# Latent attention: rotated score products on two row halves, the rotation's last sum on GpSimd, scores by pairs of heads in four banks

## The reference, cut to what matters

```
cq = rms_norm(x @ w_dq, q_norm_g)
q = (cq @ w_uq).reshape(b, s, H, MLA_NOPE + MLA_ROPE)      # H 8, NOPE 128, ROPE 64
ckv_kr = x @ w_dkv
ckv = rms_norm(ckv_kr[..., :MLA_KV_LORA], kv_norm_g)
kv = (ckv @ w_ukv).reshape(b, s, H, MLA_NOPE + MLA_V)
k_nope, v = kv[..., :MLA_NOPE], kv[..., MLA_NOPE:]
q_rope = apply_rope(q[..., MLA_NOPE:], cos[:, None, :], sin[:, None, :])
k_rope = apply_rope(ckv_kr[..., MLA_KV_LORA:], cos, sin)
sc = (einsum('bqhd,bkhd->bhqk', qn, k_nope) + einsum('bqhr,bkr->bhqk', qr, k_rope)) * scale
p = softmax(sc, -1)
o = einsum('bhqk,bkhd->bqhd', p, v)
out = o.reshape(b, s, H * MLA_V) @ w_o
```

## Time and profile before

| | us |
|---|---|
| median of 3 runs | 1151.84 |
| lowest, highest | 1151.42, 1151.96 |
| the profiled execution | 1151.98 |
| its span in the profile | 1150.2 |
| latent attention, scores to the output projection's first matmul | 53.48 to 75.81 |

### The profile page before, as it was taken

One profiled execution on the slowest core, in us unless ns is written; L12 is line 12 of the kernel. 1 busy time (PEld: TensorE's weight loads), 2 busy tenths in 40 slices (PEclk: granted clock), 3 DMA queues, 4 the chain that ended last, 5 costly groups with the idle time before them and its releaser, 6 DMA issues.

```text
span 1150.2 us, 19057 instructions
## 1 busy us (share of the span) xinstructions
PE 1135.3 (99%) x6617; PEld 981.3 (85%) x6617; DVE 804.2 (70%) x1230; ACT 700.7 (61%) x1233; POOL 50.9 (4%) x73
## 2 busy tenths in 40 slices
PE   9999999999999999999999999999999999999997
PEld 7987888888899878888888888888998888888886
DVE  5866888888756578888886655656657657655655
ACT  6665766766566666676665555556585655555553
POOL 0100000000100000000001000000000320000000
PEclk9999999999999999999999999999999999999999
DMA  7705666756344455666654765655783005876761
GB/s 247 247 7 149 186 200 199 217 179 214 128 130 148 164 147 174 211 205 195 202 176 133 216 205 171 208 151 139 217 269 121 2 21 163 231 206 171 205 156 63
DMA packets 237173, 194.75 MB, mean 169 GB/s; under 512 B 11230, under 2 KB 219712, under 8 KB 237120
## 3 DMA queue, kind: packets, MB, share of 16 engines
q1 hardware_dynamic: 237040, 194.01, 56.2%
q10 hardware_dynamic: 80, 0.03, 0.0%
HBM read 192.97 MB, written 1.05 MB: 169 GB/s over the span
## 4 chain that ended last, share of the span: by engine, by line
PE 94%; DVE 3%; ACT 1%; POOL 1%; issue 1%; DMA 0%; POOLq 0%; DVEq 0%; ACTq 0%
PE psum L853 26%; PE psum L858 14%; PE psum L884 7%; PE psum L887 7%; PE psum L891 7%; PE psum L667 6%; PE psum L669 6%; PE psum L668 6%; PE psum L723 1%; PE psum L1388 1%; DVE resid_eps L2119 1%; PE psum L841 1%; POOL st L584 1%; PE psum L1136 1%; PE psum L845 1%; PE psum L842 1%
## 5 line engine op out<-in xcount | busy, mean ns | idle before, releaser
L853 PE MATMUL psum<-act_hl,hi_u 128*128 128x512 f32 x1312 | 326.5, 391 | 0.0
L2041 DVE TENSOR_TENSOR lo_u<-raw_u,hi_u 128x2048 fp32r<-128x2048 f32 x103 | 236.1, 2292 | 93.0 <-ACT hi_u L1493 54.4
L853 PEld LDWEIGHTS psum<-act_hl,hi_u 128*128 128x128 f32 x1312 | 240.6, 188 | 46.2
L858 PEld LDWEIGHTS psum<-act_hl,lo_u 128*128 128x128 f32 x1312 | 179.0, 190 | 12.8
L858 PE MATMUL psum<-act_hl,lo_u 128*128 128x256 f32 x1312 | 183.0, 282 | 0.0
L1613 ACT ACTIVATE arena<-psum 128x256 f32<-128x256 f32 x174 | 64.9, 377 | 123.6 <-PE psum L858 114.2
L2180 DVE TENSOR_TENSOR arena<-psum,arena 128x256 f32<-128x256 f32 x174 | 73.0, 422 | 93.7 <-ACT arena L1613 93.3
L1511 ACT ACTIVATE hi_u<-raw_u 128x2048 fp32r<-128x2048 f32 x68 | 129.7, 1907 | 11.7 <-DMA raw_u<-in_ffn_w_gu 11.7
L2046 DVE TENSOR_TENSOR lo_d<-raw_d,hi_d 128x1024 fp32r<-128x1024 f32 x88 | 106.7, 1216 | 8.6 <-ACT hi_d L1520 8.6
L2190 DVE SCALAR_TENSOR_TENSOR arena<-arena,vecs 128x255 f32<-128x255 f32 x176 | 85.0, 483 | 37.9 <-ACT arena L1621 26.8
L2013 DVE TENSOR_TENSOR lo_u<-raw_u,hi_u 128x1024 fp32r<-128x1024 f32 (+6 forms) x84 | 78.2, 971 | 28.2 <-ACT hi_u L1490 28.0
(11 more groups left out here) (311 smaller groups left out, 1811.8 us busy)
## 6 DMA issues: line engine op xcount, KB each, us to landing
raw_u<-in_ffn_w_up SPq DMA_DIRECT2D x88, 512.0 KB, 5.6
raw_d<-in_ffn_w_down SPq DMA_DIRECT2D x86, 512.0 KB, 3.4
raw_u<-in_ffn_w_gu SPq DMA_DIRECT2D x84, 512.0 KB, 5.7
raw_u<-in_diff_w_qkv SPq DMA_DIRECT2D x24, 512.0 KB, 4.5
raw_u<-in_w_in SPq DMA_DIRECT2D x24, 512.0 KB, 4.5
raw_u<-in_mla_w_o SPq DMA_DIRECT2D x8, 512.0 KB, 4.5
raw_u<-in_diff_w_o SPq DMA_DIRECT2D x8, 512.0 KB, 3.9
raw_u<-in_w_out SPq DMA_DIRECT2D x8, 512.0 KB, 4.5
```

Source lines behind the costliest of these rows:

```text
L853: pe.matmul(o, hi[:, k, :], act_hl[:, k].rearrange("p a t -> p (a t)"), start=k == 0, stop=False)
L858: mm = pe.matmul(o[:, SEQ:], lo[:, k, :], act_hl[:, k, 0, :], start=False, stop=k == KC - 1)
L2041: dve.tensor_tensor(v[0], v[1], v[2].bitcast(F32), ALU.subtract).then_inc(S("lo_u_done"), 1)
```

## The change

- The rows of `m_qr` are now ordered by head first: rows 0 to 63 are the even head of a pair, rows 64 to 127 the odd one. The shared rotated keys stand in one tile `m_kr` with a copy in each half. The zeros, their memset on DVE and three of ACT's four copies are gone.
- The rotated products have 64 rows each (`m_qr[r, ...]`, `m_kr[r, :]`) and alternate between the two halves, with the results of the two heads in two banks.
- The rotation's sum moves from DVE to GpSimd. It is cut into four pieces of 32 rows for each of the four steps, since the pieces change their rows; each piece waits for the one before. DVE waits for GpSimd before it overwrites the buffers `t1` and `t2` two steps later. PE waits for DVE's three products (`m_qr_parts`) where it waited for the sum, and for all 16 pieces ahead of the first scores.
- `scores` makes two heads at once: first four products with `m_q`, then four half-height ones. The banks are 0, 1, 2, 7 instead of 0, 1, 2. PE's loop becomes: scores of pair `p`, `turn(2p-2)`, `values(2p-3)`, `turn(2p-1)`, `values(2p-2)`. The loops of DVE and ACT still go head by head in the order given above.

```diff
-        m_kr = ar(3072, 2, SEQ)
+        m_kr = ar(3072, SEQ)
+        m_bank = [0, 1, 2, 7]
...
+            pool.wait_ge(S("slopes"), 8)
+            for i in range(4):
+                pool.wait_ge(S("m_qr_parts"), 3 * i + 3)
+                t1, t2 = qr2[:, i % 2, 0], qr2[:, i % 2, 1]
+                for h in range(2):
+                    for j in range(2):
+                        src, dst = (slice(at, at + 32) for at in (64 * j + 32 * h, 64 * h + 32 * j))
+                        pool.tensor_tensor(m_qr[dst, i, :], t1[src], t2[src], ALU.add).then_inc(S("m_qr_out"), 1)
+                        pool.wait_ge(S("m_qr_out"), 4 * i + 2 * h + j + 1)
...
-                def scores(h):
-                    if h >= 3:
-                        pe.wait_ge(S("m_exp"), 2 * (h - 2))
+                def scores(p):
+                    if p >= 2:
+                        pe.wait_ge(S("m_exp"), 4 * (p - 1))
+                    o = lambda h, t: psum[:, m_bank[h % 4], t * SEQ:t * SEQ + SEQ]
+                    for h in range(2 * p, 2 * p + 2):
+                        for t in range(TT):
+                            pe.matmul(o(h, t), m_q[:, h, tok(t)], m_k[:, h, :], start=t == 0, stop=False)
                     for t in range(TT):
-                        o = psum[:, h % 3, t * SEQ:t * SEQ + SEQ]
-                        pe.matmul(o, m_q[:, h, tok(t)], m_k[:, h, :], start=True, stop=False)
-                        mm = pe.matmul(o, m_qr[:, h // 2, tok(t)], m_kr[:, h % 2, :], start=False, stop=True)
-                    mm.then_inc(S("m_scores"), 1)
+                        for e in range(2):
+                            r = slice(ROPE * e, ROPE * e + ROPE)
+                            mm = pe.matmul(o(2 * p + e, t), m_qr[r, p, tok(t)], m_kr[r, :], start=False, stop=t == 1)
+                            if t:
+                                mm.then_inc(S("m_scores"), 1)
...
-                pe.wait_ge(S("memsets"), 3)
+                pe.wait_ge(S("m_qr_out"), 16)
-                for i in range(H):
-                    scores(i)
-                    if i == 2:
+                for p in range(H // 2):
+                    scores(p)
+                    if p == 0:
                         pe.wait_ge(S("m_k_out"), 2)
                         pe.wait_ge(S("m_v_out"), 2)
-                    if i >= 2:
-                        turn(i - 2)
-                    if i >= 3:
-                        values(i - 3)
+                    else:
+                        turn(2 * p - 2)
+                        if p >= 2:
+                            values(2 * p - 3)
+                        turn(2 * p - 1)
+                        values(2 * p - 2)
...
-                        for e in range(2):
-                            for r in (slice(32 * e, 32 * e + 32), slice(64 + 32 * e, 96 + 32 * e)):
-                                act.activation(m_kr[r, e, :], psum[r, 3, 0:SEQ], ACT.Copy).then_inc(S("m_kr_out"), 1)
+                        act.activation(m_kr, psum[:, 3, 0:SEQ], ACT.Copy).then_inc(S("m_kr_out"), 1)
...
-                        dve.wait_ge(S("m_qr_out"), i - 1)
+                        dve.wait_ge(S("m_qr_out"), 4 * (i - 1))
...
-                    ch.wait()
-                    dve.tensor_tensor(m_qr[:, i, :], t1, t2, ALU.add).then_inc(S("m_qr_out"), 1)
```

More of the change, by code:

```diff
@@ L381, in program @@
         kr3 = normed[:].rearrange("p a b -> p (a b)")[:, 1280:1664].rearrange("p (a t n) -> p a t n", a=3, t=TT)
-        kr_twice = normed[:].rearrange("p a b -> p (a b)")[:, 1664:1920].rearrange("p (t c e n) -> p t c e n", t=TT, c=2, e=2)
+        kr_twice = normed[:].rearrange("p a b -> p (a b)")[:, 1664:1920].rearrange("p (t e c n) -> p t c e n", t=TT, c=2, e=2)
+        kr_rows = normed[:].rearrange("p a b -> p (a b)")[:, 1664:1920].rearrange("p (t n) -> p t n", t=TT)
         qr2 = masks[:].rearrange("p (i a b) t -> p i a (b t)", i=2, a=2)
@@ L972, in mla @@
                     if i >= 2:
-                        pe.wait_ge(S("m_qr_out"), i - 1)
+                        pe.wait_ge(S("m_qr_parts"), 3 * (i - 1))
                     high_products(*turned[:1], u, *turned[1:], 0, [0], True)
@@ L994, in mla @@
                         for t in range(TT):
-                            mm = pe.transpose(psum[:, 3, t * P:t * P + P], kr_twice[:, t].rearrange("p c e n -> p (c e n)"), ident[:])
+                            mm = pe.transpose(psum[:, 3, t * P:t * P + P], kr_rows[:, t, :], ident[:])
                         mm.then_inc(S("latent_tr"), 1)
@@ L1004, in mla @@
                     if i == 0:
-                        pe.wait_ge(S("m_kr_out"), 4)
+                        pe.wait_ge(S("m_kr_out"), 1)
                     else:
                         pe.wait_ge(S("m_q_out"), 4)
-                        pe.wait_ge(S("m_qr_out"), 4)
+                        pe.wait_ge(S("m_qr_parts"), 12)
                     keys = [psum[:, 4 * i + h // 2, (h % 2) * SEQ:(h % 2) * SEQ + SEQ] for h in range(4)]
@@ L1750, in mla @@
                         for t in range(TT):
-                            act.activation(m_p[:, i % 3, t, :], psum[:, i % 3, t * SEQ:t * SEQ + SEQ], ACT.Exp,
+                            act.activation(m_p[:, i % 3, t, :], psum[:, m_bank[i % 4], t * SEQ:t * SEQ + SEQ], ACT.Exp,
                                            scale=M_SCALE, bias=soft[:, i, 1, t:t + 1],
@@ L2288, in mla @@
                     if i >= 2:
-                        dve.wait_ge(S("m_qr_out"), i - 1)
+                        dve.wait_ge(S("m_qr_out"), 4 * (i - 1))
                     dve.wait_ge(S("used_u"), U_UQ + i + 1)
                     raw = psum[:, 5 + 2 * (i % 2), 0:SEQ]
-                    ch.put(dve.tensor_tensor(t1, raw, ropeq[:, 0, :], ALU.mult))
+                    dve.tensor_tensor(t1, raw, ropeq[:, 0, :], ALU.mult).then_inc(S("m_qr_parts"), 1)
                     for c in range(2):
                         src, dst = slice(64 * c, 64 * c + 64), slice(64 - 64 * c, 128 - 64 * c)
-                        ch.put(dve.tensor_tensor(t2[dst], raw[src], ropeq[src, 1, :], ALU.mult))
-                    ch.wait()
-                    dve.tensor_tensor(m_qr[:, i, :], t1, t2, ALU.add).then_inc(S("m_qr_out"), 1)
+                        dve.tensor_tensor(t2[dst], raw[src], ropeq[src, 1, :], ALU.mult).then_inc(S("m_qr_parts"), 1)
                     split_u(U_UQ + i + 2)
@@ L2308, in mla @@
                         dve.wait_ge(S("m_scores"), i + 1)
-                        ch.link(dve.tensor_reduce(soft[:, i, 0, 0:2], psum[:, i % 3, :].rearrange("p (t k) -> p t k", t=2),
+                        ch.link(dve.tensor_reduce(soft[:, i, 0, 0:2], psum[:, m_bank[i % 4], :].rearrange("p (t k) -> p t k", t=2),
                                                   AX, ALU.max))
@@ L2574, in _ @@
             dve.memset(resid_eps[:, :, D:], ROOT_D * EPS ** 0.5).then_inc(S("memsets"), 1)
-            dve.memset(m_kr, 0.0).then_inc(S("memsets"), 1)
             norm_first()
```

1 line of the change is left out of this document (removed).

## The result

| | before | after |
|---|---|---|
| median, us | 1151.68 | 1155.51 (1154.98 to 1155.69) |
| span of the profiled execution | 1150.2 | 1153.2 |
| scores' first to output projection's first matmul | 22.33 | 24.23 |
| first scores wait for GpSimd | none | 1.30 |

The changed kernel takes 1.0031 times as long as the one before, with a 95% interval from 1.0022 to 1.0040: **3.8 us slower**. That is outside the predicted range, which ended at 1154.2. The two profiled executions (1151.98 and 1154.98) differ by 3.0 us.

The account below looks back on a forecast made before the run. PE bounds the score stretch: waits of 3.91 us, less 0.3 of old waits and 2.64 saved on products, give +0.97, taken as +1.0, with GpSimd's sum and the projections at 0. From 1151.84: 1152.8 us, range 1150.9 to 1154.2.

Parts of the forecast that it names:

- GpSimd's sum: Rotation's sum on GpSimd: 16 pieces at 0.72 us each, hidden by the projections, so costing nothing.
- Stretched by 1.51/1.05: GpSimd's pieces beside a busy DVE: 1.00 us each, ending at 51.6, before PE's need at 53.4.
- the threshold of 1.11: GpSimd's pieces: above 1.11 us each, (53.4 - 35.6)/16, the cover by the projections is gone.
- The row: Trace of a 512-element GpSimd addition, 1.05 us beside idle DVE and 1.51 beside busy, used for the pieces' stretch.
- GpSimd's sum is late: Rival before the first scores: pieces exclude DVE's splits or exceed 1.11 us, 3.4 us late, 1156.2 us; chance 0.10.
- all 9.7 us of splits: DVE's two-input splits up to 53.4 us; full exclusion would leave GpSimd 8.1 us for 11.5 of pieces.
- The products: Half-height rotated products in the scores: 1.07 us a pair in place of 1.73, saving 2.64 over four pairs.
- The 0.21 us that I charged for going in and out: Scores of each pair: 0.21 us lost entering and leaving the half-height form, included in the 1.07.
- 0.97: Lower bound for a pair's half-height products, half of the second layer's 1.93 us; takes 0.3 off the time.
- The waits: PE's waits for DVE and ACT in the paired scores' stage: 3.91 us in all, against 0.3 before.
- turn(1): PE's transposes of head 1, after DVE scales it: start at 60.84 after a wait of 1.17 us.
- The projections: Stage before the scores: GpSimd's work slows DVE's splits within slack, so 0, bounds -0.2 and +0.5 us.

Follow-up runs that it names:

- fine_waits: The changed kernel, with scores of each pair waiting only for that pair's GpSimd pieces instead of all 16; 1153.75 us, ratio 1.0017.
- turned_first: The changed kernel, with DVE scaling the odd head before the next maximum and ACT copying turned probabilities before the next even head's exponentials; 1153.84 us, ratio 1.0017.
- gpsimd_only: The kernel before, with only the rotation's sum moved to GpSimd, as one 128-row addition a step in the old row order; 1151.91 us, ratio 0.9999.

## Why the prediction was wrong, point by point

1. **GpSimd's sum: the step that failed.** "Stretched by 1.51/1.05 it is 1.00 each, to 51.6: still in time." The piece by itself was nearly right, though by a guess between two rows: 0.72 with its wait, 0.73 and 0.08 of wait measured. Sixteen of them would have ended at 47.9. The stretch was not right. Two of GpSimd's additions in the kernel after, beside DVE's products from PSUM:

```profile
L632 POOL TENSOR_TENSOR arena<-masks x2: 731/736/740, 41.0 to 41.8; 32x256 f32<-32x256 f32 x2
```

Three more, and the splits that each of them meets, from the timelines of POOL and DVE:

```profile
42.58 1.70 POOL L632 TENSOR_TENSOR arena<-masks 32x256 f32<-32x256 f32 x1
44.36 1.59 POOL L632 TENSOR_TENSOR arena<-masks 32x256 f32<-32x256 f32 x1
51.15 1.60 POOL L632 TENSOR_TENSOR arena<-masks 32x256 f32<-32x256 f32 x1
...
42.47 1.23 DVE L2029 TENSOR_TENSOR lo_u<-raw_u,hi_u 128x1024 fp32r<-128x1024 f32 x1
43.61 1.76 DVE L2029 TENSOR_TENSOR lo_u<-raw_u,hi_u 128x1024 fp32r<-128x1024 f32 x1
...
50.84 1.31 DVE L2029 TENSOR_TENSOR lo_u<-raw_u,hi_u 128x1024 fp32r<-128x1024 f32 x1
```

Beside a long split a piece takes 2.2 to 2.4 times as long, not 1.44 times. The mean came to 1.21 us against the threshold of 1.11 that the prediction itself had worked out. The row was a bad bound: an addition of 512 columns, which had run for 0.80 us when DVE's one instruction with two inputs in SBUF began beside it (889.87 and 890.67). The cost was 1.46 us (54.56 less 53.10) where I had 0, and fine_waits gives 1.76 back and measures 1153.75, inside the predicted range: without this step the time lies inside it. The rival "GpSimd's sum is late" held 0.10 and 3.4 us. It came with under half of that.
The Trainium skill (SBUF — State Buffer, Who interferes with whom) says that such a pair of instructions contends and that the lock is exclusive. What stretched the 1.51 us stays open, but the lines above agree with the rule. The three pieces start 0.11, 0.75 and 0.31 us behind the split that they meet. They end at 44.28, 45.95 and 52.75, each 0.58 to 0.60 us after that split has ended (43.70, 45.37 and 52.15), and so do the other three pieces that meet a long split. So such a piece stands until the split is over, whenever it came, and then needs little less than its 0.73 us. A split that comes while a piece works waits in turn: 1.76 us in place of the 1.22 of before, and two of them 2.90 (42.47 to 45.37) in place of 2.35, as in the timeline of DVE before:

```profile
42.41 2.35 DVE L2013 TENSOR_TENSOR lo_u<-raw_u,hi_u 128x1024 fp32r<-128x1024 f32 x2
```

The loss came out under half of the rival's because the rival took all 9.7 us of splits from GpSimd. The pieces were busy for 18.23 us, 6.6 more than 16 x 0.73. Of these 6.6 us, 5.5 lie in the six pieces beside long splits and the rest beside the short ones.

2. **The products: right inside, mis-sized outside.** The 64-row group takes 1.07 us, as taken from the earlier trace rows. But the 128-row block beside it takes 1.82 to 1.93 instead of 1.73, because each change of form costs on both sides. The scores of the four pairs take 2.96, 2.99, 2.89 and 2.89 us in the kernel after, 0.53 more in all than four times 2.80 (0.08 of it is the first block, behind its wait for GpSimd). The 0.21 us that I charged for going in and out are 0.35. The Trainium skill (TensorE: Matmul & The Clock Gate, Part 3) has a pack at the price of one matmul; by my estimate that was some 0.85 us a pair. The overlap itself agrees with it (4 x 0.216 = 0.86). The price of the form comes on top, so a pair's products cost 1.21, not 0.85. Two sums of the prediction were wrong here: 0.85 in place of 1.07 lowers the time by 0.9 us over four pairs, not 0.5, and 0.97 lowers it by 0.4, not 0.3. Neither moves the forecast.

3. **The waits: right in kind, place and nearly in size.** From start to start, measured and predicted: `turn(1)` 1.33 and 1.17, later odd transposes 0.41 and 0.42 against 0.46, even values 0.38 each against 0.38, `turn(6)` 0.52 against 0.53. `turn(0)` did not wait (0.15 predicted). What I had left out is that PE loses about 0.1 us more behind a wait (values 0.96 to 0.97 instead of 0.86), and 0.05 in the transposes behind a half-height group (0.49 instead of 0.44). All together 4.33 against 3.91. turned_first shows the cause by experiment: with the scaling and the copy ahead, the waits in the rounds go but for 0.22.

4. **The sum of the stage.** 22.33 - 0.3 of old waits - 2.11 of products + 4.33 = 24.25, and 24.23 stands in the profile. Predicted was +1.0, measured +1.90: 0.53 from point 2, 0.42 from point 3. With 1.46 from point 1 this makes 3.4 of the 3.8 us.

5. **The projections.** I set 0, with bounds of -0.2 and +0.5. From the start of GpSimd's tables to the first scores' turn it took 53.48 - 30.47 = 23.01 us before, and 53.10 - 29.92 = 23.18 after. In gpsimd_only, with one addition a step, it took 55.16 - 32.15 = 23.01 again. So the sixteen pieces cost 0.2 us here, by DVE's slowed splits, and the move itself nothing. The remaining 0.2 us of the difference are within the spread of the runs.

## What to carry to other kernels

- Less work on the busiest engine shortens the time only as far as no wait takes its place. First write the orders of all engines so that PE never waits (here with two other products, or a pair's scores, between a result and its use), then count the saving. Here the changed products and banks came out 3.8 us slower in the old orders, and 1.9 us faster in new ones with finer waits.
- Work moved to an idle engine needs a deadline for each piece. Let the consumer wait for the pieces that it uses, not for all of them, and price them beside the neighbour's real instructions. An addition on GpSimd cost per instruction here, not per row: one of 128 rows took 0.83 us, and four of 32 rows take 3.2 even undisturbed (4 x 0.73 and 4 x 0.08).

## What the runs showed of the hardware that I had not expected

- The two row halves of TensorE run side by side over at least four instructions each: order within the group is free (20.10 against 20.07 us), but both halves must be used (23.49).
- Going into 64-row products and back costs 0.35 to 0.40 us of PE's path, about half of it in the 128-row instructions around them. The weight load idles 0.33 us at each change.
- An addition on GpSimd of 32 x 256 takes 0.73 us beside DVE instructions that read PSUM and 1.6 to 1.75 beside ones with two inputs in SBUF. A piece that meets a running split of 128 x 1024 ends 0.6 us after the split does, whenever it came, and such a split that meets a running piece takes 1.76 in place of 1.22.
